# A down projection summed in device memory instead of on chip: ten chunks, accumulating transfers, four staging tiles

## What is computed

```python
def conv_ffn(h, w_up, conv_w, conv_b, w_down):
    up = depthwise_conv(h @ w_up, conv_w, conv_b, FFN_CONV // 2)
    g, v = jnp.split(up, 2, axis=-1)
    return (jax.nn.gelu(g, approximate=True) * v) @ w_down
...
hx2 = modulate(rms_norm(x, g_ffn_pre[l]), sh2, sc2)
x = x + gt2 * rms_norm(conv_ffn(hx2, ...), g_ffn_post[l])
```

## Time and profile before

| | |
|---|---|
| Median of three runs | 2106.05 us (2102.48 to 2106.25) |
| Profiled execution | 2105.41 us, span 2103.6 us |
| Granted clock of PE, mean | 0.996 |
| Mean transfer rate | 148 GB/s |
| Read and written in device memory | 300.95 MB, 8.39 MB |

### The profile page before, as it was taken

How to read it: one execution, slowest core, us unless ns; L and a number is a source line. 1 busy time by engine, 2 the same in 40 slices (tenths; PEclk the granted TensorE clock), 3 DMA queues, 4 the chain that set the end, 5 groups by cost and what they waited for, 6 DMA issues and landing times.

```text
span 2103.6 us, 28297 instructions
## 1 busy us (share of the span) xinstructions
PE 2071.2 (98%) x11682; PEld 1772.5 (84%) x11682; DVE 1529.6 (73%) x2202; ACT 811.6 (39%) x1077; POOL 78.7 (4%) x145
## 2 busy tenths in 40 slices
PE   7999999999999999999999999999999999999998
PEld 4678887888777888888889898898988889888887
DVE  5567978876988975867767676676766758577577
ACT  5346577543323442423324233332333424233243
POOL 0000000001110000000000000000000000000002
PEclk9999999999999999999999999999999999999999
DMA  9953424434876523333333333334233333232343
GB/s 394 408 204 110 154 96 161 137 109 173 323 277 225 181 90 134 100 128 111 110 130 101 138 103 103 129 101 140 100 120 121 100 130 100 91 101 101 100 172 109
DMA packets 86193, 311.19 MB, mean 148 GB/s; under 512 B 9456, under 2 KB 13552, under 8 KB 84016
## 3 DMA queue, kind: packets, MB, share of 16 engines
q1 hardware_dynamic: 67824, 243.09, 32.7%
q0 software_dynamic: 17424, 65.50, 9.1%
q10 hardware_dynamic: 816, 0.79, 0.1%
HBM read 300.95 MB, written 8.39 MB: 147 GB/s over the span
## 4 chain that ended last, share of the span: by engine, by line
PE 80%; DVE 2%; ACT 1%; DMA 1%; issue 0%; DVEq 0%; ACTq 0%
PE bank L988 26%; PE bank L990 26%; PE bank L989 26%; DMA w_raw<-in_stream 1%; PE bank L1099 1%; DVE acc L2167 0%; PE bank L1284 0%; DVE w_lo L1532 0%; ACT w_hi L602 0%; PE bank L1313 0%; PE bank L1194 0%; DVE acc L2139 0%; ACT lru_u L698 0%; DVE cv L1544 0%; DVE x L2193 0%
## 5 line engine op out<-in xcount | busy, mean ns | idle before, releaser
L988 PE MATMUL bank<-h_hi,w_hi 128*128 128x512 f32 (+1 forms) x1968 | 711.2, 361 | 4.2 <-ACT y_lru L671 1.2
L989 PE MATMUL bank<-h_lo,w_hi 128*128 128x512 f32 (+1 forms) x1968 | 708.6, 360 | 0.0
L990 PE MATMUL bank<-h_hi,w_lo 128*128 128x512 f32 (+1 forms) x1968 | 707.2, 359 | 0.0
L1532 DVE TENSOR_TENSOR w_lo<-w_raw,w_hi 128x1024 fp32r<-128x1024 f32 x260 | 316.0, 1222 | 157.9 <-ACT w_hi L602 157.8
L988 PEld LDWEIGHTS bank<-h_hi,w_hi 128*128 128x128 f32 x1968 | 372.3, 189 | 63.6 <-issue 11.9
L602 ACT ACTIVATE w_hi<-w_raw 128x1024 fp32r<-128x1024 f32 x260 | 273.0, 1056 | 389.1 <-DMA w_raw<-in_stream 389.0
L990 PEld LDWEIGHTS bank<-h_hi,w_lo 128*128 128x128 f32 x1968 | 372.1, 189 | 56.6
L989 PEld LDWEIGHTS bank<-h_lo,w_hi 128*128 128x128 f32 x1968 | 372.3, 189 | 49.0
L988 PE MATMUL bank<-act_hi,w_hi 128*128 128x512 f32 (+1 forms) x688 | 265.0, 385 | 1.7 <-DVE acc L2139 1.5
L990 PE MATMUL bank<-act_hi,w_lo 128*128 128x512 f32 (+1 forms) x688 | 264.2, 384 | 0.0
L989 PE MATMUL bank<-act_lo,w_hi 128*128 128x512 f32 (+1 forms) x688 | 264.2, 384 | 0.0
(11 more groups left out here) (340 smaller groups left out, 2711.4 us busy)
## 6 DMA issues: line engine op xcount, KB each, us to landing
w_raw<-in_stream SPq DMA_DIRECT2D x340, 512.0 KB, 3.5
ada_raw<-in_adabg POOLq DMA_DIRECT2D x112, 512.0 KB, 4.3
ada_raw<-in_ada SPq DMA_DIRECT2D x64, 512.0 KB, 13.5
x<-in_x_t SPq DMA_DIRECT2D x4, 1024.0 KB, 8.4
acc<-in_adabg SPq DMA_DIRECT2D x8, 512.0 KB, 6.1
x<-in_x_t POOLq DMA_DIRECT2D x4, 1024.0 KB, 9.4
x_kept_d<-x SPq DMA_DIRECT2D x4, 1024.0 KB, 5.6
c<-in_ctx_t SPq DMA_DIRECT2D x2, 1024.0 KB, 14.3
```

The costliest lines, as they stand in the source:

```text
L988: t.matmul(out, w, v, start=start, stop=False)
L989: t.matmul(out, w, v_l, start=False, stop=False)
L990: return t.matmul(out, w_l, v, start=False, stop=stop)
L1532: v.tensor_tensor(lo_unit(n), raw_unit(n), hi_unit(n).bitcast(F32), ALU.subtract).then_inc(lo_done, 1)
```

## The change

- ACT, not DVE, empties the banks of `down(0)` to `down(9)`: `take_down` copies the bank into tile m mod 4 of `acc`, which now serves as a ring of four. Before it copies, it waits until the transfer of four tiles earlier has finished. The roundings of the units d+4 to d+10 are placed between the copies.
- POOL issues a transfer for each tile (`add_down`): chunk 0 is written to a new tensor in device memory, chunks 1 to 9 are added to it by the transfer. The loads of the modulation blocks are placed between them.
- SP brings the finished sum back (`load_sums`), four transfers of 1 MB, ahead of the load of unit D+4. `add_last` waits for its quarter.
- Two groups of semaphores serve both purposes and get new names (`quarter_in`, `tile_moved`).

```diff
+            def load_sums():
+                for i in range(4):
+                    sp.wait_ge(tile_moved[i], 16 + 16 * ((NCH - 1) * KT // 4))
+                for i in range(4):
+                    sp.dma_start(acc[:, ds(4 * i * L, 4 * L)].rearrange("p (k l) -> p k l", k=4), acc_d[:, 4 * i:4 * i + 4, :]).then_inc(quarter_in[i], 16)
+
...
             for n in range(SLOT0 + 4 * HEADS + 4, UNITS):
+                if n == UNITS - KEPT:
+                    load_sums()
                 load_unit(n)
...
-            load_ada(ADA_LOAD[4], len(COLS) * KT)
+            def add_down(c, m):
+
+                pool.wait_ge(down_added, c * KT + m + 1)
+                if c == 0:
+                    pool.dma_start(acc_d[:, m, :], tile(acc, m % 4)).then_inc(tile_moved[m % 4], 16)
+                else:
+                    pool.wait_ge(tile_moved[m % 4], 16 + 16 * ((c * KT + m) // 4))
+                    pool.dma_start(acc_d[:, m, :], tile(acc, m % 4), accum_op=ALU.add).then_inc(tile_moved[m % 4], 16)
+
+            block = FFN_ADA * KT + 1
+            load_ada(ADA_LOAD[4], block)
+            for c in range(NCH - 1):
+                for m in range(KT):
+                    add_down(c, m)
+                    if m % 4 == 2 and c in ADA_CHUNKS and block < len(COLS) * KT:
+                        load_ada(block, block + 1)
+                        block += 1
...
+            def take_down(c, m):
+
+                act.wait_ge(down_done, c * KT + m + 1)
+                if c * KT + m >= 4:
+                    act.wait_ge(tile_moved[m % 4], 16 + 16 * ((c * KT + m) // 4))
+                a.activation(tile(acc, m % 4), bank[4 + m % 4][:, :], ACT.Copy).then_inc(down_added, 1)
+
...
                         gelu_of(n)
-                        hi(*range(d + 4, d + 11))
+                        for m in range(KT):
+                            take_down(c - 1, m)
+                            if m in (2, 4, 6, 8, 10, 13, 15):
+                                hi(d + 4 + (2, 4, 6, 8, 10, 13, 15).index(m))
...
-            def add_down(c, m):
-                dve.wait_ge(down_done, c * KT + m + 1)
-                if c == 0:
-                    v.tensor_copy(tile(acc, m), bank[4 + m % 4][:, :]).then_inc(down_added, 1)
-                else:
-                    v.tensor_tensor(tile(acc, m), tile(acc, m), bank[4 + m % 4][:, :], ALU.add).then_inc(down_added, 1)
...
                         for m in range(KT):
-                            add_down(c - 1, m)
                             if m in (3, 5, 7, 9, 11):
...
                 dve.wait_ge(down_done, c * KT + i + 1)
+                dve.wait_ge(quarter_in[m // 4], 32)
                 v.tensor_tensor(tile(acc, m, a0, a1), tile(acc, m, a0, a1), bank[m % 4][:, 0:a1 - a0], ALU.add).then_inc(down_added, 1)
```

More of the change, by code:

```diff
@@ L163, in wait, with build @@
         self.eng.wait_ge(self.sem, self.k)
-def build(nc, x1_d, x_t, ctx_t, par_d, late_d, stream, ada0, adabg, gates_d, tabs_d, wf_d, out_t):
+def build(nc, x1_d, acc_d, x_t, ctx_t, par_d, late_d, stream, ada0, adabg, gates_d, tabs_d, wf_d, out_t):
     ctx = ExitStack()
@@ L368, in build @@
         par_in, pos_in, late_in = sem("par_in"), sem("pos_in"), sem("late_in")
-        x_in, c_in = [sem(f"x_in{i}") for i in range(4)], [sem(f"c_in{i}") for i in range(2)]
-        x1_in = [sem(f"x1_in{i}") for i in range(4)]
+        quarter_in, c_in = [sem(f"quarter_in{i}") for i in range(4)], [sem(f"c_in{i}") for i in range(2)]
+        tile_moved = [sem(f"tile_moved{i}") for i in range(4)]
         x1_kept, x1_in_again = sem("x1_kept"), sem("x1_in_again")
@@ L468, in load_a0 @@
                 sp.dma_start(ada0_raw[:, u % A0SLOTS, :], ada0[u]).then_inc(a0_in[u % A0SLOTS], 16)
-            sp.dma_start(x0[:, 0:4, :], x_t[:, 0:4, :]).then_inc(x_in[0], 16)
+            sp.dma_start(x0[:, 0:4, :], x_t[:, 0:4, :]).then_inc(quarter_in[0], 16)
             sp.dma_start(pos0[:, :], late_d[:, NCONV:NLATE]).then_inc(pos_in, 16)
@@ L473, in _ @@
             for i in range(1, 4):
-                sp.dma_start(x0[:, 4 * i:4 * i + 4, :], x_t[:, 4 * i:4 * i + 4, :]).then_inc(x_in[i], 16)
+                sp.dma_start(x0[:, 4 * i:4 * i + 4, :], x_t[:, 4 * i:4 * i + 4, :]).then_inc(quarter_in[i], 16)
             for i in range(2):
@@ L576, in _ @@
             for i in range(4):
-                pool.dma_start(x1[:, 4 * i:4 * i + 4, :], x_t[:, 4 * i:4 * i + 4, :]).then_inc(x1_in[i], 16)
+                pool.dma_start(x1[:, 4 * i:4 * i + 4, :], x_t[:, 4 * i:4 * i + 4, :]).then_inc(tile_moved[i], 16)
                 load_ada(ADA_LOAD[i], ADA_LOAD[i + 1])
-            load_ada(ADA_LOAD[4], len(COLS) * KT)
+            def add_down(c, m):
[13 more added lines that the diff above has]
+                        block += 1
             pool.wait_ge(x1_in_again, 32)
@@ L1579, in _ @@
             for k in range(0, KT, 4):
-                dve.wait_ge(x_in[k // 4], 16)
+                dve.wait_ge(quarter_in[k // 4], 16)
                 v.tensor_tensor(*positions(x0, pos0, k, 4), ALU.add).then_inc(x_posed, 1)
@@ L1870, in place @@
             def place(i):
-                dve.wait_ge(x1_in[i // 2], 16)
+                dve.wait_ge(tile_moved[i // 2], 16)
                 v.tensor_tensor(*positions(x1, late_par, 2 * i, 2), ALU.add).then_inc(x_posed, 1)
@@ L2310 @@
     kept = nc.dram_tensor("x1_kept_d", (P, KT, L), F32, kind="Internal").ap()
-    build(nc, kept, *args, out)
+    summed = nc.dram_tensor("down_summed_d", (P, KT, L), F32, kind="Internal").ap()
+    build(nc, kept, summed, *args, out)
     r = run_bass_kernel_spmd(nc, [arrays], core_ids=[0])
```

## The result

The changed kernel takes 2116.81 us (median of six runs, 2114.12 to 2123.24), the kernel before 2105.89 us in the same comparison (six runs, 2102.48 to 2108.47): ratio 1.0055, 95% interval 1.0042 to 1.0068, 0.5% slower (10.9 us between the medians, 11.6 by the ratio). The forecast was 2114.6 us, slower.

A forecast was written before the change was run, and what follows sets the result against it. PE, busy 1250.00 of 1250.00 us from 787 to 2037 us, was taken as the bound. Terms 0 + 0 + 0 + 0 + 8.6 on 2105.4 gave 2114.0, with the offset 2114.6 us; range 2106 to 2150.

The forecast's parts named there:

- Parts 1 and 2: Chunks: 110 us of DVE work removed and 96 us of copies added on ACT, both worth 0 beside busy PE.
- Part 3, the loop: Four-tile ring: copy, issue and flight take 6.7 of 10.9 us allowed, flight limit 9.7 us; value 0.
- the slack at the chunk's end: End of each chunk: two tiles less a copy, 4.8 us, covering 4.5 us of delay from the slowest flights.
- Part 3, the rate: Down stages: at most 0.91 MB per tile takes 2.4 of 2.72 us at 381 GB/s, fitting narrowly; value 0.
- Part 4: POOL and DVE queues in down stages: nothing late, unit loads may slow from 3.5 to 6.9 us; value 0.
- rival B: Ten chunks: accumulating traffic slows unit loads to 8.9 us, PE waits for lo of d+9; +20, 2134.6 us; chance 0.15.
- still leaves 1.8 us: Argument against slow unit loads stopping PE in the down stages: loads took up to 5.1 us, PE waits from 6.9.
- Part 5: Tail: 4 MB of sums ahead in SP's queue delay the last kept unit from 2046.1 to 2055.9; +8.6 us.
- A: Tail, the forecast itself: only the kept units are late, 2113 to 2117 us; chance 0.56.
- C: Chunks: accumulation slow in throughput, 3.8 us per tile against 2.72; +117 us, 2231 us; chance 0.12.
- D: Tail: sums don't hold back kept units, which land before 2047.5; not slower, 2106 us; chance 0.12 with its like.

The follow-up runs named there:

- both repairs together: Changed kernel with sums loaded during the last chunk's third pair and lo parts of d+9 made before block sums of d+10: 2106.73 us, ratio 0.9999.
- The experiment with x1 ahead: Kernel before, without accumulating transfers, its two 2 MB reloads of x1 moved ahead of the four kept units: 2114.40 us, ratio 1.0033.
- the early sums: Changed kernel with one 1 MB load of the sums ahead of each unit of the last chunk's third pair: 2109.82 us, ratio 1.0014.
- lo parts first: Changed kernel with DVE making the lo parts of d+9 before the block sums of d+10 in every down stage: 2114.83 us, ratio 1.0039.
- plain writes: Changed kernel with its 144 accumulating transfers turned into plain writes, each chunk overwriting the one before: 2111.11 us, ratio 1.0028.

## Why the prediction was right

- **Parts 1 and 2** (DVE's relief and ACT's copies are worth 0): right. The copy measured 598 ns; both repairs together give 0.9999, and moving the copies back to DVE changes nothing.
- **Part 3, the loop** (6.7 of 10.9 us): right in size. From the start of a copy to the landing of its tile the 144 accumulating ones took 6.9 us in the median, and PE never waited for a bank, not even with each tile moved twice. The sum added POOL's issue to a flight that contains it; without that the limit for a flight lies higher than 9.7 us. The 144 flights took 3.9 to 10.0 us. One loop took 11.5 us of the 10.9 allowed, and nothing came of it, as the slack at the chunk's end said.
- **Part 3, the rate and Part 4** (a unit load may slow from 3.5 to 6.9 us; value 0): the mechanism was right, the term not. The forecast put 0 and gave the slow unit loads to rival B at 15%. They did come: in the changed kernel unit d+10, for which DVE waits there, took 3.5, 8.0, 7.4, 8.9, 7.0, 5.3, 6.4, 5.8, 5.2 and 5.2 us in the ten stages, and PE waited in the three with 7.4 us or more, 1.04, 0.36 and 1.92 us, at exactly the place named, for the lo parts of d+9. Other units took up to 8.1 us in later stages and stopped nobody. So the limit of 6.9 us held within a few tenths, for this one unit. It is B with a smaller price, three chunks instead of ten in this execution: 3.3 us of waits and 1.7 of half clock (below) of the 5.8 lost; the remaining 0.8 us I have not placed. The step that failed is "still leaves 1.8 us": I had set the loads at the 5.1 us of today, though the transfers were to be so much denser.
- **Part 5** (+8.6 us from the place of 4 MB in SP's queue): right, as a mechanism and nearly in size. The last kept unit was forecast to land at 2055.9 on the scale of before, 19.0 us after the last `pair_sums` (2036.9). Its rounding began with its landing at 2065.29, 18.5 us after that of the changed kernel (2046.8). The first square came 7.9 us late instead of 8.6, the end 8.0. The half microsecond under it fits the rate: 401 to 430 GB/s in the slices of 2048 to 2062 against the 381 assumed. The second half of x1 landed 29.1 us after the last `pair_sums`, as forecast (2066 on the scale of before). The experiment with x1 ahead shows nearly the same loss without the change.
- **Sum.** 8.6 for the tail and 0 for the middle were 8.0 and about 3. The total lies 2 us above the forecast, inside A's 2113 to 2117, though A said that only the kept units are late: that it still fits owes something to luck, as the tail came out under its term and rival B's cost was small. The middle is the term that the sum put at 0 and was short of.
- **Rivals.** C (throughput) was priced at 117 us with a chance of 0.12. The doubled transfers show that it was far off: not even they make PE wait for a bank. D is out: the kept units landed 18.5 us after the last `pair_sums` and not before 10.6, and with the sums behind them they landed after 8.8 and the loss of the tail shrank from 8.0 to 1.3 us.

## What to carry to other kernels

PE was busy 1250 of 1250 us, and taking work from its neighbours was worth nothing; in such a stretch look for what the new transfers push aside. The dearest thing here was not the 160 accumulating transfers but four loads placed ahead of others in one queue at the moment when all of them were released together: large loads that are not needed first go earlier or behind. And where an engine works through a written order, a step whose data is ready should not stand behind one that waits for a transfer: here that order set how slow the load of unit d+10 could be.

## What the runs showed that I had not expected

**PE's clock.** After its wait of 1.92 us, which ended at 1219.4, PE ran at half its rate for 3.4 us (granted clock 0.50, the lower of the levels 1.2 and 2.4 GHz), and from 2063, in its wait of 5.58 us in the tail, the clock was 0.50 for 10.2 us; after waits of 1.04 and 1.10 us (chunk 1 here, chunk 5 with the early sums) it stayed at 1.00. Busy times by 2 us, the granted clock in the third column from the end:

```profile
1217.00:1219.00 2.00, 0.46 (x3) 0.04 (x1) 2.00 (x3) 1.67 (x2) 0.00 (x0) 1.00 1.08 335
1219.00:1221.00 2.00, 1.62 (x9) 1.65 (x10) 2.00 (x3) 1.59 (x3) 0.00 (x0) 0.70 0.98 289
1221.00:1223.00 2.00, 2.00 (x11) 2.00 (x10) 1.38 (x2) 0.00 (x0) 0.00 (x0) 0.50 0.24 94
```

So the wait of 1.92 us moved the chunk by 3.8 us, twice its length: 1.9 for the wait and 1.7 for the half clock. In the changed kernel's tail the half clock cost next to nothing: from the first square to the end it took 55.2 us, and 55.1 before. Where it lasted 13.7 us (lo parts first, and every tile moved twice) that stretch took 56.1 us in both.

**The share of the transfer engines.** Accumulating raised it from 0.74 to 0.99 at nearly the same counted bytes (235 and 229 GB/s), and still a quarter more bytes fitted (290 instead of 229 GB/s). The page counts 305.14 MB read in the changed kernel and as many with plain writes, so whatever accumulation reads of the old sums is not in the bytes read; it shows in the share and in the flights. Here a share near 1 told that transfers take longer, not that none can be added: with each tile moved twice the page's median flight of a tile went from 5.7 to 7.3 us and that of the unit loads of the stage from 6.8 to 7.3.
